# A two-block transformer kernel: where the squares of its norms are added up

## What is computed

```
def rmsnorm(x, g):
    y = x * lax.rsqrt(jnp.mean(x * x, axis=-1, keepdims=True) + eps)
    return y * g

# first part, layer i
h = modulate(rmsnorm(x, norm_mix_g[i]), sh1, sc1)
x = x + g1 * (pool_mixer(h) if i == 0 else sgu_mixer(h))
h = modulate(rmsnorm(x, norm_mlp_g[i]), sh2, sc2)
x = x + g2 * (square(relu(h @ w1)) @ w2)
x = rmsnorm(x, final_g)                      # after both layers
# second part
proj = rms_norm(x, norm_mix_pre) @ w_in
mix = concat([attention(q, k, v), rwkv7(p)]) @ w_out
x = x + rms_norm(mix, norm_mix_post)
f = conv_gated_ffn(rms_norm(x, norm_ffn_pre))
x = x + rms_norm(f, norm_ffn_post)
```

## Time and profile before

| | |
|---|---|
| median of 3 runs | 1975.54 us (1975.31 to 1977.28) |
| the profiled execution | 1977.91 us, of which its span 1976.5 us |
| TensorE busy | 1820.3 us (92%) |
| VectorE busy | 1051.8 us (53%) |
| ScalarE busy | 647.4 us (33%) |
| mean granted TensorE clock | 0.945 of 2.4 GHz |

### The profile page before, as it was taken

One profiled execution on the slowest core, in us unless ns is written; L12 is line 12 of the kernel. 1 busy time (PEld: TensorE's weight loads), 2 busy tenths in 40 slices (PEclk: granted clock), 3 DMA queues, 4 the chain that ended last, 5 costly groups with the idle time before them and its releaser, 6 DMA issues.

```text
span 1976.5 us, 21469 instructions
## 1 busy us (share of the span) xinstructions
PE 1820.3 (92%) x8828; PEld 1467.6 (74%) x8828; DVE 1051.8 (53%) x1336; ACT 647.4 (33%) x798; POOL 82.6 (4%) x87
## 2 busy tenths in 40 slices
PE   5659999999899899999999989967499999999997
PEld 2238888888678688888886868846388888888885
DVE  4874675467545543244345574453656542566523
ACT  2123312321333342134334423433344431244412
POOL 2400010001000000000000101100000000000000
PEclk8669999999899899999998989988699999999997
DMA  9713375257222223232322420002032332323221
GB/s 356 282 64 107 119 245 169 90 188 239 80 88 84 85 86 106 86 107 86 106 91 69 97 69 4 4 1 85 22 107 94 98 95 98 102 90 106 87 85 43
DMA packets 124000, 208.55 MB, mean 106 GB/s; under 512 B 13965, under 2 KB 48421, under 8 KB 123904
## 3 DMA queue, kind: packets, MB, share of 16 engines
q1 hardware_dynamic: 115424, 174.94, 27.3%
q0 software_dynamic: 7808, 29.43, 4.5%
q10 hardware_dynamic: 672, 2.82, 0.4%
HBM read 204.01 MB, written 4.73 MB: 106 GB/s over the span
## 4 chain that ended last, share of the span: by engine, by line
PE 87%; DVE 8%; ACT 1%; DMA 1%; issue 1%; SPq 1%; DVEq 0%; ACTq 0%
PE bank L531 74%; DVE ada_acc L1672 2%; DMA ada_ring<-in_ada_w 1%; PE bank L898 1%; PE bank L547 1%; PE bank L881 1%; PE bank L861 1%; SPq L476 1%; PE bank L542 1%; DVE gT L2015 1%; PE bank L618 1%; DVE outer L2013 0%; PE bank L943 0%; PE bank L673 0%; PE bank L922 0%
## 5 line engine op out<-in xcount | busy, mean ns | idle before, releaser
L1597 DVE TENSOR_TENSOR w_lo<-raw,w_hi 128x2048 fp32r<-128x2048 f32 x138 | 316.2, 2292 | 503.4 <-ACT w_hi L1160 503.4
L1160 ACT ACTIVATE w_hi<-raw 128x2048 fp32r<-128x2048 f32 x138 | 263.8, 1912 | 606.7 <-PE bank L531 584.7
L531 PE MATMUL bank<-u_hi,w_hi 128*128 128x512 f32 x768 | 300.5, 391 | 0.8 <-DVE conv L2271 0.8
L531 PE MATMUL bank<-u_hi,w_lo 128*128 128x512 f32 x768 | 299.0, 389 | 0.0
L531 PE MATMUL bank<-u_lo,w_hi 128*128 128x512 f32 x768 | 298.8, 389 | 0.0
L531 PE MATMUL bank<-h_hi,w_hi 128*128 128x512 f32 x736 | 291.8, 396 | 5.1 <-DVE h_lo L1644 5.1
L531 PE MATMUL bank<-h_lo,w_hi 128*128 128x512 f32 x736 | 288.6, 392 | 0.0
L531 PE MATMUL bank<-h_hi,w_lo 128*128 128x512 f32 x736 | 288.5, 392 | 0.0
L531 PE MATMUL bank<-f_hi,w_hi 128*128 128x512 f32 x512 | 200.4, 391 | 2.4 <-DVE f_lo L1647 2.4
L531 PE MATMUL bank<-f_lo,w_hi 128*128 128x512 f32 x512 | 199.9, 390 | 0.0
L531 PE MATMUL bank<-f_hi,w_lo 128*128 128x512 f32 x512 | 199.7, 390 | 0.0
(11 more groups left out here) (351 smaller groups left out, 2038.6 us busy)
## 6 DMA issues: line engine op xcount, KB each, us to landing
raw<-in_mlp_w SPq DMA_DIRECT2D x128, 512.0 KB, 4.5
raw<-in_w_ffn_up SPq DMA_DIRECT2D x64, 512.0 KB, 4.5
ada_ring<-in_ada_w POOLq DMA_DIRECT2D x24, 1024.0 KB, 5.9
ada_ring<-in_ada_w SPq DMA_DIRECT2D x9, 2048.0 KB, 13.2
raw<-in_w_ffn_down SPq DMA_DIRECT2D x32, 512.0 KB, 4.4
raw<-in_w_in SPq DMA_DIRECT2D x20, 512.0 KB, 4.4
raw<-in_sgu_w_in SPq DMA_DIRECT2D x16, 512.0 KB, 4.9
x_rows<-in_ada_w SPq DMA_DIRECT2D x3, 2048.0 KB, 11.8
```

What stands on the lines that cost most here:

```text
L531: mm = te.matmul(bank[:, n], a, b, start=first and k == 0 and j == 0, stop=last and k == 3 and j == 2)
L1160: se.activation(m.ring(s)[0], m.raw[:, slot], ACT.Copy).then_inc(sem("hi_made"), 1)
L1597: ve.tensor_tensor(lo, m.raw[:, slot], hi.bitcast(F32), ALU.subtract).then_inc(sem("lo_made"), 1)
```

## The change

It has four parts.

1. Projection: ScalarE copies `first_rstd` ahead of the split of slab `first + 3`.
2. Tails of MIX1, MLP1 and LAST: VectorE's additions of tiles 4, 5 and 6 stand between the evictions of the last group. The square of tile 7 is no longer added by VectorE; `norm_mean` takes four products over the sum and four over that square (`LAST_APART`). POST has this split too, and there ScalarE squares tiles 4 to 7 out of PSUM ahead of copying them.
3. FFN: no additions on VectorE. ScalarE squares into eight places, and TensorE takes four products over each (`norm_mean_of_all`).
4. The other norms keep their additions; only the start flag of their products differs.

The words that came with the change also speak of v's columns standing first in the gating unit. The diff has nothing on it: the slabs of `sgu_w_in` have the order (2, 3, 0, 1) in both kernels, and the order on SyncE is the same.

```diff
--- before.py
+++ after.py
@@ -141,7 +141,7 @@
 
 NORM_MIX0, NORM_MLP0, NORM_MIX1, NORM_MLP1, NORM_FINAL, NORM_POST, NORM_FFN, NORM_LAST = range(8)
 ADDED_ON_POOL = (NORM_MIX0,)
-ADDED_ON_DVE = (NORM_MLP0, NORM_MIX1, NORM_MLP1, NORM_FINAL, NORM_POST, NORM_FFN, NORM_LAST)
+ADDED_ON_DVE = (NORM_MLP0, NORM_MIX1, NORM_MLP1, NORM_FINAL, NORM_POST, NORM_LAST)
 NORM_PROJ = "proj"
 NORMED = {NORM_MLP0: 0, NORM_MIX1: 1, NORM_MLP1: 2, NORM_PROJ: 3, NORM_FFN: 4}
 
@@ -389,11 +389,20 @@
         return self.ada_ring[:, n] if n < ADA_RING - 1 else self.x_rows[:, :, :].rearrange("p j (a n) -> p (j a) n", a=2)
 
 
+LAST_APART = (NORM_MIX1, NORM_MLP1, NORM_POST, NORM_LAST)
+SUMMED_ON_PE = (NORM_FFN,)
+
+
+def additions(norm):
+
+    return 6 if norm in LAST_APART else 7
+
+
 def added(norm, k):
 
     if norm in ADDED_ON_POOL:
         return "pool_added", 7 * ADDED_ON_POOL.index(norm) + k
-    return "dve_added", 7 * ADDED_ON_DVE.index(norm) + k
+    return "dve_added", sum(additions(n) for n in ADDED_ON_DVE[:ADDED_ON_DVE.index(norm)]) + k
 
 
 def slab_sources(t):
@@ -535,11 +544,27 @@
                 after_n(n)
         mm.then_inc(sem("slab_used"), 1)
 
-    def norm_mean(norm, total):
-        name, count = added(norm, 7)
+    def norm_mean(norm, squares):
+
+        name, count = added(norm, additions(norm))
         te.wait_ge(sem(name), count)
+        apart = norm in LAST_APART
         for j in range(4):
-            mm = te.matmul(bank[:, 4, j:j + 1], total[:, P * j:P * j + P], m.mean_ones[:, 0:1], start=True, stop=True)
+            mm = te.matmul(bank[:, 4, j:j + 1], squares[:, 3, P * j:P * j + P], m.mean_ones[:, 0:1], start=j == 0, stop=not apart,
+                           skip_group_check=True)
+        if apart:
+            te.wait_ge(sem("squared"), 8 * norm + 8)
+            for j in range(4):
+                mm = te.matmul(bank[:, 4, j:j + 1], squares[:, 0, P * j:P * j + P], m.mean_ones[:, 0:1], start=False, stop=True,
+                               skip_group_check=True)
+        mm.then_inc(sem("meaned"), 1)
+
+    def norm_mean_of_all(norm, squares):
+        for k in range(DT):
+            te.wait_ge(sem("squared"), 8 * norm + k + 1)
+            for j in range(4):
+                mm = te.matmul(bank[:, 4, j:j + 1], squares[:, k, P * j:P * j + P], m.mean_ones[:, 0:1], start=k == 0 and j == 0,
+                               stop=k == DT - 1, skip_group_check=True)
         mm.then_inc(sem("meaned"), 1)
 
     def norm_spread(norm):
@@ -591,7 +616,7 @@
         mm.then_inc(sem("ada_summed"), 1)
 
     ada_row(1)
-    norm_mean(NORM_MIX0, m.pooled[:, 3])
+    norm_mean(NORM_MIX0, m.pooled)
     ada_sum(0)
     ada_sum(2)
     norm_spread(NORM_MIX0)
@@ -662,7 +687,7 @@
                     if beside:
                         beside(8 * half + 4 * g + k)
         if next_norm:
-            norm_mean(next_norm, sq[:, 3])
+            norm_mean(next_norm, sq)
 
     ada1 = {"summed": 0}
 
@@ -679,7 +704,7 @@
         ada1_sum(sum(2 - i % 2 for i in range(w)))
 
     te.wait_ge(sem("mod_made"), 11)
-    norm_mean(NORM_MLP0, m.sq_b[:, 3])
+    norm_mean(NORM_MLP0, m.sq_b)
     mlp(0, NORM_MLP0, NORM_MIX1, m.u_hi, m.u_lo, m.sq_b, ada1_beside)
     ada1_sum(ADA1_LOADS)
     norm_spread(NORM_MIX1)
@@ -747,13 +772,13 @@
     mix_head(5)
     two_slabs("sgu_out", 0, m.g_hi, m.g_lo, gated, beside=last_heads)
     two_slabs("sgu_out", 1, m.g_hi, m.g_lo)
-    norm_mean(NORM_MLP1, m.sq_c[:, 3])
+    norm_mean(NORM_MLP1, m.sq_c)
     mlp(1, NORM_MLP1, None, m.u2_hi, m.u2_lo, m.sq_d)
 
 
 
     def two_means():
-        norm_mean(NORM_FINAL, m.sq_d[:, 3])
+        norm_mean(NORM_FINAL, m.sq_d)
         te.wait_ge(sem("second_added"), 7)
         for j in range(4):
             mm = te.matmul(bank[:, 4, 4 + j:5 + j], m.first_rstd[:, P * j:P * j + P], m.mean_ones[:, 0:1], start=True, stop=True)
@@ -1105,9 +1130,9 @@
             slab(s + k, group, m.m_hi[:, 4 * k:4 * k + 4], m.m_lo[:, 4 * k:4 * k + 4], k == 0, k == 1,
                  before_k if g == 0 else None, before_n, k_outer=g == 0 and k == 0)
     squares = m.ar[:, :, :, :].rearrange("p i a t -> p (i a) t")
-    norm_mean(NORM_POST, squares[:, 3])
+    norm_mean(NORM_POST, squares)
     norm_spread(NORM_POST)
-    norm_mean(NORM_FFN, squares[:, 3])
+    norm_mean_of_all(NORM_FFN, squares)
     norm_spread(NORM_FFN)
 
 
@@ -1134,7 +1159,7 @@
                     te.wait_ge(sem("f_lo_made"), 16 * half + 4 * k + kk + 1)
                 slab(s + k, group, m.u3_hi[:, 4 * k:4 * k + 4], m.u3_lo[:, 4 * k:4 * k + 4], k == 0, k == 3,
                      before_k if g == 0 else None, before_n, k_outer=g == 0 and k == 0)
-    norm_mean(NORM_LAST, m.conv[:, 3])
+    norm_mean(NORM_LAST, m.conv)
     norm_spread(NORM_LAST)
     for k in range(DT):
         te.wait_ge(sem("x_finished"), k + 1)
@@ -1171,6 +1196,9 @@
             se.wait_ge(sem("slab_used"), last_slab + 1)
 
     def square(norm, k, src, squares):
+        if norm in SUMMED_ON_PE:
+            se.activation(squares[:, k], src, ACT.Square).then_inc(sem("squared"), 1)
+            return
         if k >= 4:
             name, count = added(norm, k - 3)
             se.wait_ge(sem(name), count)
@@ -1398,9 +1426,9 @@
     se.activation(m.zT[0:64, 0], m.zT[0:64, 0], ACT.Tanh).then_inc(sem("z_squashed"), 1)
     se.activation(m.zT[:, 1], m.zT[:, 1], ACT.Sigmoid).then_inc(sem("z_squashed"), 1)
     normed_hi(range(4, 8))
-    split_to(first + 3)
     se.wait_ge(sem("spread"), NORM_FINAL + 1)
     se.activation(m.first_rstd, m.rstd_bank, ACT.Copy).then_inc(sem("first_copied"), 1)
+    split_to(first + 3)
     decays()
     split_to(first + 4)
     empty(1, range(4))
@@ -1528,10 +1556,9 @@
                     square(NORM_POST, o, m.mixed[:, o], squares)
         for n in range(4):
             full(s + 1, group, n)
+            if g:
+                square(NORM_POST, 4 + n, bank[:, n], squares)
             se.activation(m.mixed[:, 4 * g + n], bank[:, n], ACT.Copy).then_inc(sem("act_emptied"), 1)
-    for o in range(4, 8):
-        emptied(GROUPS["w_out"] + 1, o - 4)
-        square(NORM_POST, o, m.mixed[:, o], squares)
     root(NORM_POST)
     for k in range(DT):
         se.wait_ge(sem("x_mixed2"), k + 1)
@@ -1791,9 +1818,11 @@
                                             op0=ALU.mult, op1=ALU.add).then_inc(sem("dve_emptied"), 1)
                     if layer and half and g:
                         gained_lo(o)
-        for o in range(4, 8):
-            add_square(next_norm, o, sq)
-            if layer:
+                    elif half and g and n:
+                        add_square(next_norm, o - 1, sq)
+        if layer:
+            for o in range(4, 8):
+                add_square(next_norm, o, sq)
                 add_second_square(o)
 
     def gained_lo(o):
@@ -1903,8 +1932,8 @@
             full(s + 1, group, n)
             ve.scalar_tensor_tensor(out=m.xT[:, o], in0=bank[:, n], scalar=m.modv(1, 2, o), in1=m.xT[:, o],
                                     op0=ALU.mult, op1=ALU.add).then_inc(sem("dve_emptied"), 1)
-    for o in range(4, 8):
-        add_square(NORM_MLP1, o, m.sq_c)
+            if g and n:
+                add_square(NORM_MLP1, o - 1, m.sq_c)
 
     mlp(1, NORM_MLP1, NORM_FINAL, lambda k: m.gain[:, 24 + k:25 + k], lambda k: m.modv(1, 3, k), m.u2_hi, m.u2_lo, m.sq_d)
     split_to(SLABS["proj"] + 1)
@@ -2239,7 +2268,7 @@
             if g and k == 0:
                 for o in range(1, 4):
                     add_square(NORM_POST, o, squares)
-    for o in range(4, 8):
+    for o in range(4, 7):
         add_square(NORM_POST, o, squares)
     inverse_and_diagonal(NORM_POST)
     ve.wait_ge(sem("spread"), NORM_POST + 1)
@@ -2249,9 +2278,6 @@
         ve.wait_ge(own.sem, n)
         ve.wait_ge(sem("x_final"), k + 1)
         ve.tensor_tensor(m.xT[:, k], m.xT[:, k], m.mixed[:, k], ALU.add).then_inc(sem("x_mixed2"), 1)
-        if k >= 2:
-            add_square(NORM_FFN, k - 1, squares)
-    add_square(NORM_FFN, 7, squares)
     inverse_and_diagonal(NORM_FFN)
     normalise_lo(NORM_FFN, m.xT, m.f_lo, m.f_hi, lambda k: m.col("norm_ffn_pre_2", k))
 
@@ -2293,8 +2319,8 @@
                     ve.tensor_copy(m.f[:, o], bank[:, n]).then_inc(sem("dve_emptied"), 1)
                 else:
                     ve.tensor_tensor(m.f[:, o], m.f[:, o], bank[:, n], ALU.add).then_inc(sem("dve_emptied"), 1)
-    for o in range(4, 8):
-        add_square(NORM_LAST, o, m.conv)
+                    if g and n:
+                        add_square(NORM_LAST, o - 1, m.conv)
     inverse_and_diagonal(NORM_LAST)
     ve.wait_ge(sem("spread"), NORM_LAST + 1)
     for k in range(DT):
```

## The result

The changed kernel took **1966.48 us** (median of 6 runs, 1963.65 to 1969.61) against 1975.86 (6 runs, 1975.31 to 1982.88) before: ratio 0.9947, with the 95% interval in brackets [0.9932, 0.9962]. That is 9.4 us less; 17.85 was forecast, and the time lies above the range. The profiled execution took 1966.12 us against 1977.91, so the two traces differ by 11.8 us, of which 2.0 are there because the profiled execution of before was that much above its own median.

What follows compares the result with a forecast made beforehand. TensorE was taken as the bound, holding 87% of the chain that ended last. Terms 6.4 + 4.4 + 2.3 + 1.45 + 2.0 + 1.3 = 17.85 us took the 1975.54 median to 1957.7, range 1953.4 to 1962.6.

Steps and rivals of the forecast that it cites:

- Part 1: Projection: earlier `first_rstd` copy starts `decays` sooner, clock stays at 2.4 GHz, slab takes 11.05 us; 6.4 us gained.
- rival B: Projection: clock falls in `decays` despite the 1.1 us rest, slab keeps 12.48 us; gain 3.6, time 1960.5; chance 0.12.
- So I see nothing that keeps the old time: Behind the projection: decays, blocks and triangular solve all count from TensorE's products, so the 6.4 us carries through.
- rival D: Slabs after norms: clock stays low longer; gains lost once stretches grow by more than 36 us; 1977.7; chance 0.02.
- Part 3: Tails: fewer additions between last eviction and mean; gains LAST 2.3, MLP1 1.45, MIX1 2.0 us.
- rival C: Three tails: the second four products run slow, losing 0.8 + 0.8 + 0.5 us; time 1959.8; chance 0.10.
- should mostly be at the upper level: LAST and MLP1 tails: products coming 2.3 us earlier run mostly at 2.4 GHz, eight taking 1.94 us.
- Part 2: POST, norm after the mixer: squares taken from PSUM before copying bring the mean's end forward; 4.4 us gained.
- the 1.0 us that I had kept for the low end: POST: about 1.0 us more if the 2.09 us spread product falls before the clock sinks and halves.
- Part 4: FFN norm: 32 products at 1.2 GHz replace VectorE's adds, mean ends at 16.2 instead of 17.5 us; gain 1.3.
- Rival A: FFN: the long gapless train warms the clock; 3.3 us less, time 1954.4; chance 0.12.
- The rule of the Trainium skill quoted in the prediction: FFN train: activity releases the slow resting clock, so 64 records would bring 2.4 GHz; term nearer 4.6 than 1.3 us.

Runs made afterwards that it cites:

- same_again: The changed kernel run once more with nothing edited; 1968.37 us, ratio 0.9948 to the kernel before.
- narrow_split: Changed kernel with key norms issued 16 and 16 records, twelve wide products apart, and spatial-weight transposes twelve wide products ahead of the rank-one products; 1965.61 us, ratio 0.9938.
- split_no_filler: Changed kernel with key norms, transposes and the two rank-one products set apart by wide products, without an unread wide product ahead of `decays`; 1962.73 us, ratio 0.9925.

## Why the prediction was half right

The parts are numbered as the prediction's paragraphs: 1 the projection, 2 POST, 3 the three tails, 4 FFN.

**Part 1, the first step that failed.** "With so short a rest I take the clock to stay at 2.4 GHz." `decays` started where forecast (1.80 us earlier than before, measured against the last wide product), but the clock fell at 1058.50, 2.7 us into it. In 8 of 9 traces of this form it fell 1.5 to 2.7 us in. So rival B was the common case and had 0.12. It was too mild as well: it let the slab keep its 12.48 us, and it took 13.49, since the low stretch now lies on wide products instead of on the wait. Measured 3.44 where 6.4 was the term and 3.6 the lower bound. (1066.67 less 1061.7 is 4.97 and not 4.95, which changes nothing.) The proof I took, `rates` right behind wide products, lacked the rest of 1.16 us, and its clock held in all traces. The rest alone doesn't decide either: in same_again the clock held with it.

**"So I see nothing that keeps the old time": the second failure, and the larger one.** I counted no cost anywhere between the edits. The traces show 1.7 us lost behind the rank-one products, 0.5 behind MLP1 and 3.2 behind the key norms, in code that the change does not touch. The nearest I had is rival D (0.02, "Nothing in the trace speaks for it"), the gains given back through the clock, but neither at these places nor as I priced it. I asked for low stretches that grow by 36 us; their sum did not grow. TensorE's clock from 500 to 1940, first of before, then of the changed kernel:

```profile
500.00:1940.00 1440.00, 1357.56 (x6891) 1114.26 (x6890) 714.21 (x855) 503.34 (x631) 26.33 (x36) 0.96 0.25 79
```

```profile
500.00:1940.00 1440.00, 1381.37 (x7007) 1137.05 (x7006) 708.59 (x848) 505.05 (x634) 26.40 (x36) 0.96 0.25 79
```

Both 0.96; cut finer, the low stretches add up to 116.0 us before and 109.2 after. What changed is what lies under a low stretch. Before, they stood mostly on waits and on the feed of a norm's first slab, where they cost little; now two of them stand on slabs, where half of their length is lost (3.42 us of it cost 1.7, 6.82 cost 3.2). At the key norms the cut shows the cause: the same products, cut in two, were followed by no fall.

Why the kernel before escapes the falls, with the same stretches in it, no run tests by itself, but the traces point at the moment. The rank-one products start 31.1 us behind the rise of the clock behind MIX1 in the changed kernel (515.78 to 546.88), and 32.8 us behind it in the kernel before (516.64 to 549.42). In the ten traces with these products uncut, the six with a fall have 30.9 to 31.8 us there, the four without 32.6, 32.8, 37.3 and 37.5. The uncut key norms start 17.8 to 18.4 us behind the rise that follows the decays in four traces with a fall, and 18.7 to 19.0 us in the four without; same_again has no such rise. So the shorter tail of MIX1, which brought the rank-one products forward by 2.54 us but the rise only by 0.86, moved them from one group into the other. This is read from traces and not set by an edit.

The cuts have to be read beside this. narrow_split and split_no_filler start their cut key norms 17.8 and 18.3 us behind that rise, where the uncut ones fell, and have no fall: there the cut did it. The cut rank-one products start at 31.9 to 32.0 us in three traces and at 37.2 in the fourth, beyond every uncut trace with a fall, so the cut and the moment are not separated. Nor are they for the filler: counted from the rise behind MLP1, the eight slow `decays` start at 383.0 to 383.9, 390.7 and 391.0 us, the three with a filler at 384.9, 385.0 and 391.2, and same_again, undisturbed without one, at 385.1.

The Trainium skill, "TensorE: Matmul & The Clock Gate", Part 1, calls the number of slow products run-variable, by the phase at the kernel's start. It speaks of the start alone; same_again shows the like for falls in the middle, where the same kernel had one fall less and another half as long, 4.4 us in the stage.

**Part 3.** MLP1 1.50 (1.45 forecast). MIX1 1.65 (2.0) and LAST 1.66 (2.3): in both the second four products were slow, 1.65 and 1.69 us instead of 1.03, because the clock fell at 502.13 and at 1942.55, inside the mean. That is rival C in two of three tails, 1.0 us short in all. My sentence was that products 2.3 us earlier "should mostly be at the upper level". They came earlier, and the clock fell among them all the same; at MLP1, where TensorE waits about as long ahead of the mean (1.44 us, and 1.38 at LAST), it fell at 662.55, behind the mean. What decides between them is not shown.

**Part 2.** 4.44 against 4.4. The spread product stayed at 2.08 us, so the 1.0 us that I had kept for the low end did not come; only the products nobody reads brought it to 1.12.

**Part 4.** 1.50 against 1.3, with the mean's end 16.0 us behind the first scaled tile against 16.2. Rival A is out:

```profile
1394.50:1408.00 13.50, 13.50 (x64) 13.50 (x64) 8.57 (x13) 4.41 (x7) 0.00 (x0) 0.50 0.00 0
```

64 one-column records without a gap, at half the clock throughout, as the earlier trace rows said. The rule of the Trainium skill quoted in the prediction, by which activity releases the clock, did not hold for these products: by it the term would have been 3.3 us too high.

**What came by itself.** 0.98 us ahead of the change and 2.0 in the mixer, where the clock was low for 6.8 us less (1160.90 to 1167.73, where before has 1161.76 to 1172.00 and 1175.42 to 1178.83). same_again has two stretches there again, 13.7 us together as before, and gains nothing in the mixer: so I count it to the execution and not to the change. Over the fourteen traces the mixer lies between 2.0 us ahead of before and 1.6 behind it. Terms of the sum in profiles: 14.2 at the sites, -5.4 between, +3.0 by chance, 11.8. The 14.2 us alone would have been 1961.3, inside the range. What the range missed is the 5.4 us lost between the sites, for which the sum had no term; 14.2 less 5.4 is 8.8, near the 9.4 of the medians.

## What to carry to other kernels

When edits of a microsecond or two shift TensorE's work, ask for each stretch of narrow products (one column, one row deep) and each short wait what stands behind it: if it is a slab of wide products, a fall of the clock there costs half of its length, and it may come though nothing in that stretch was edited, because its moment moved. Cutting such a stretch in two, with wide products between, cost 0.05 us at the key norms and gave 3.2. For the wait of 1.2 us, one product ahead of `decays` went with 2.7 us less in the traces, but may not be what gave them; take two or three traces before you credit such an edit. And in a train of products bound by TensorE, take products off its end with an engine that has just gone idle: it gave 1.5 us, where GpSimd's additions at the front gave nothing.
